# Two layers of mixed attention on one core: values projected with 512 weight columns per matmul, and half of each layer's memory values projected inside the two 16-head attentions

## The reference, cut to what matters

```python
m = rms_norm_2(mem, mem_norm_g)
for layer in range(DEPTH):
    ...
    h = h + memory_cross_attention(rms_norm_2(h, xa_norm_g[layer]), m, ...)

def memory_cross_attention(h, m, wq, wkv, wo):
    kv = m @ wkv
    k = kv[..., :D].reshape(B, -1, XA_HEADS, XA_HEAD_DIM)
    v = kv[..., D:].reshape(B, -1, XA_HEADS, XA_HEAD_DIM)
```

## Time and profile before

| | us |
|---|---|
| median of 3 runs | 1078.62 (1078.27 to 1079.88) |
| the profiled execution | 1080.66 |
| its span in the trace | 1078.9 |
| PE busy | 1039.4 (96%) |
| DVE busy | 693.4 (64%) |
| ACT busy | 535.6 (50%) |

### The profile page before, as it was taken

One profiled execution on the slowest core, in us unless ns is written; L12 is line 12 of the kernel. 1 busy time (PEld: TensorE's weight loads), 2 busy tenths in 40 slices (PEclk: granted clock), 3 DMA queues, 4 the chain that ended last, 5 costly groups with the idle time before them and its releaser, 6 DMA issues.

```text
span 1078.9 us, 19922 instructions
## 1 busy us (share of the span) xinstructions
PE 1039.4 (96%) x8144; PEld 1004.7 (93%) x8144; DVE 693.4 (64%) x1002; ACT 535.6 (50%) x822; POOL 226.1 (21%) x167
## 2 busy tenths in 40 slices
PE   8969999999999999999999999999999999999996
PEld 8959987999998899979999999899999999999996
DVE  5989976674446567646455658846576655658842
ACT  4325567365548546355435437644345545436631
POOL 3745201210004232001000103611024100102610
PEclk9979999999999999999999999999999999999998
DMA  9424532555540344515443455446545542555421
GB/s 347 154 86 146 196 118 88 186 195 195 195 162 35 121 155 178 217 58 194 167 147 109 170 190 194 154 169 245 205 164 209 181 156 81 193 190 180 148 106 39
DMA packets 26623, 173.27 MB, mean 161 GB/s; under 512 B 2880, under 2 KB 5184, under 8 KB 5952
## 3 DMA queue, kind: packets, MB, share of 16 engines
q1 hardware_dynamic: 24832, 161.26, 41.8%
q10 hardware_dynamic: 1728, 11.14, 2.7%
HBM read 167.15 MB, written 5.24 MB: 160 GB/s over the span
## 4 chain that ended last, share of the span: by engine, by line
PE 75%; DVE 13%; ACT 5%; issue 2%; POOL 2%; DMA 1%; SPq 0%; POOLq 0%; DVEq 0%; ACTq 0%
PE bank L373 63%; DVE wl L1163 5%; PE bank L479 2%; DVE work L1193 2%; DVE work L1477 2%; ACT wh L737 2%; PE bank L509 1%; POOL acc L1603 1%; DMA vec<-vecs 1%; DVE work L1480 1%; PE bank L499 1%; PE bank L441 1%; PE bank L511 1%; PE bank L600 1%; ACT work L1084 1%
## 5 line engine op out<-in xcount | busy, mean ns | idle before, releaser
L1163 DVE TENSOR_TENSOR wl<-raw,wh 128x1024 fp32r<-128x1024 f32 x300 | 394.9, 1324 | 251.0 <-ACT wh L737 249.3
L737 ACT ACTIVATE wh<-raw 128x1024 fp32r<-128x1024 f32 x300 | 312.9, 1054 | 302.9 <-PE bank L373 286.1
L373 PE MATMUL bank<-xh,wh 128*128 128x256 f32 x1312 | 367.3, 287 | 6.2 <-DVE wl L1163 4.1
L373 PE MATMUL bank<-xh,wl 128*128 128x256 f32 x1312 | 363.0, 283 | 0.0
L373 PE MATMUL bank<-xl,wh 128*128 128x256 f32 x1312 | 339.2, 284 | 0.0
L373 PEld LDWEIGHTS bank<-xh,wh 128*128 128x128 f32 x1312 | 252.1, 192 | 7.8 <-DVE wl L1163 4.8
L373 PEld LDWEIGHTS bank<-xh,wl 128*128 128x128 f32 x1312 | 252.3, 192 | 0.2
L373 PEld LDWEIGHTS bank<-xl,wh 128*128 128x128 f32 x1312 | 237.9, 192 | 0.1
L373 PE MATMUL bank<-yh,wh 128*128 128x256 f32 x768 | 210.6, 287 | 0.8 <-ACT yh L1088 0.8
L373 PE MATMUL bank<-yh,wl 128*128 128x256 f32 x768 | 208.5, 284 | 0.0
L373 PE MATMUL bank<-yl,wh 128*128 128x256 f32 x768 | 179.8, 285 | 4.2 <-POOL yl L1638 4.2
(11 more groups left out here) (156 smaller groups left out, 1307.3 us busy)
## 6 DMA issues: line engine op xcount, KB each, us to landing
raw<-w SPq DMA_DIRECT2D x149, 1024.0 KB, 4.8
k_scratch<-kt ACTq DMA_DIRECT2D x2, 1024.0 KB, 7.1
kt<-k_scratch ACTq DMA_DIRECT2D x2, 1024.0 KB, 6.3
cs<-cst SPq DMA_DIRECT2D x1, 1152.0 KB, 12.8
raw<-w SPq DMA_DIRECT2D x2, 512.0 KB, 6.3
h<-xt SPq DMA_DIRECT2D x1, 1024.0 KB, 7.2
v<-memt ACTq DMA_DIRECT2D x1, 1024.0 KB, 6.4
m_scratch<-yh ACTq DMA_DIRECT2D x1, 1024.0 KB, 6.1
```

Of the source, the lines that this page charges most:

```text
L373: return pe.matmul(b[:, j, :], lhs, rhs, start=k0 + k == 0 and q == 0 and (j == 0 or not both_open), stop=k0 + k == KT * p.deep - 1 and q ...
L737: act.activation(wh[:, n % 2, :, part], raw[:, n % RAW_SLOTS, :, part], ACT.Copy).then_inc(hi_ready, 1)
L1163: dve.tensor_tensor(wl[:, n % 2, :, part], raw[:, n % RAW_SLOTS, :, part], wh[:, n % 2, :, part].bitcast(F32), ALU.subtract).then_inc(lo_r ...
```

## The change

A new `project_tokens` takes all the phases that have tokens on partitions. Their weight chunks hold 512 rows by 512 columns instead of 1024 by 256. A matmul has the same stationary operand (128 tokens) and moves 512 weight columns, into a whole PSUM bank; a chunk has 24 of them. Both banks of the pair fill together (one for each 128 tokens), after two chunks. The halves of a chunk are now two row tiles each, both in the slot's layout and in what is waited for: the first half can be used when it alone is ready, and `w_used` rises after each half. ACT reads out one bank at a time. The second 512 columns of `va` and `vb` go to the same two banks, so their first matmul in a bank waits for that bank's read-out.

Columns 0 to 511 of the memory values of layer 0 and 1 become phases `vm0` and `vm1` of two chunks each. `project_piece` issues their 48 matmuls three at a time, one piece in each of the 16 turns of attention A and B, between the transposes (or the sums) and the values. ACT and DVE make the four halves (`filled_in`) in turns 2, 4, 8, 12 and 3, 5, 9, 13. ACT reads the result out at turns 18 and 19, sends it to DRAM (`v_scratch`, 512 KB each), and fetches it back before the cross attention. `oa` and `ob` now wait for that read-out in `enter`. `vx0` and `vx1` keep two chunks each, and the early read-out of `vx1` (`first_values`) is gone.

The very first weight chunk's two half transfers are contiguous in each partition (4 KB) instead of pieces of 512 bytes.

```diff
+            def project_tokens(name, oh, ol, ready=None, hooks={}, tile0=0):
+                p = PH[name]
+                enter(p)
+                for c in range(p.n):
+                    n = p.n0 + c
+                    slot = n % 2
+                    for half in range(2):
+                        pe.wait_ge(lo_ready, 2 * n + half + 1)
+                        if ready is not None and c < 2:
+                            hi_, lo_ = ready(4 * c + 2 * half)
+                            pe.wait_ge(*hi_)
+                            pe.wait_ge(*lo_)
+                        for t in range(2):
+                            if c >= 2 and c % 2 == 0 and half == 0:
+                                pe.wait_ge(evac[p.reader], p.base + c - 1 + t)
+                            for e in range(2):
+                                k = 4 * (c % 2) + 2 * half + e
+                                kk, part = tile0 + k, slice(t * P, t * P + P)
+                                for q in range(3):
+                                    mm = pe.matmul(bank[p.pair + t][:, :], (oh, oh, ol)[q][:, kk, part],
+                                                   (wh, wl, wh)[q][:, slot, half, e * 2 * CW:(e + 1) * 2 * CW],
+                                                   start=k == 0 and q == 0, stop=k == KT - 1 and q == 2,
+                                                   skip_group_check=True)
+                            if t == 1:
+                                mm.then_inc(w_used, 1)
+                            elif half == 1 and c % 2 == 1:
+                                mm.then_inc(tok_full, 1)
+                            if (c, half, t) in hooks:
+                                hooks[c, half, t]()
```

```diff
@@ TensorE, attention A @@
                     if 2 <= t < heads + 2:
                         turn(t - 2)
+                    if filler is not None and t < heads + 2:
+                        project_piece(filler, t - 2, yh, yl, KT)
                     if t == 3:
@@ TensorE, attention B @@
                 if 2 <= t < NH + 2:
                     z_sums(t - 2)
+                if t < NH + 2:
+                    project_piece("vm1", t - 2, yh, yl, KT)
@@ ScalarE @@
+            def filled_in(name, t):
+                p = PH[name]
+                for h_, at in ((2, 2), (3, 4), (4, 8), (5, 12)):
+                    if t == at:
+                        hi(2 * p.n0 + h_)
+                if t == 18:
+                    if name == "vm1":
+                        act.wait_ge(z_sp, NH)
+                    act.wait_ge(tok_full, TOKBASE[name] + 1)
+                    half_values(name, 0)
+                if t == 19:
+                    act.wait_ge(w_used, 2 * (p.n0 + p.n))
+                    half_values(name, 1)
+                    act.wait_ge(act_evac, p.end)
+                    act.dma_start(v_scratch[int(name[2])], v_half.rearrange("p t n -> p (t n)")).then_inc(v_saved, 16)
@@ ScalarE, values of A @@
-            def va(c, b):
-                if c == 2:
+            def va(c, t, b):
+                if c == 1 and t == 0:
                     spread("mem", rb_m)
@@ VectorE @@
+            def filled_in(name, t):
+                for h_, at in ((2, 3), (3, 5), (4, 9), (5, 13)):
+                    if t == at:
+                        lo(2 * PH[name].n0 + h_)
```

More of the change, by code:

```diff
@@ L77, in schedule, with add @@
     order = []
-    def add(name, chunks, reader, outs=None, deep=1):
+    def add(name, chunks, reader, outs=None, deep=1, wide=False):
         nonlocal at
@@ L86, in add @@
         count[reader] += p.outs
+        p.wide = wide
         p.pair = 2 * (len(order) % 2)
@@ L133 @@
 PH, NCHUNK = schedule()
+HALF = KT * P
 def bases(*uses):
@@ L142, in bases @@
     return table
+TOKBASE = bases(("va", 2), ("vm0", 1), ("vb", 2), ("vm1", 1), ("zf", 1), ("vn", 1), ("vx0", 1), ("vx1", 1))
 XBASE = bases(*[(u, 4) for u in ("first", "B", "mix0", "xa0", "ffn0", "mix1", "xa1", "ffn1")])
@@ new lines, in project_piece @@
+            def project_piece(name, i, oh, ol, tile0):
+                p = PH[name]
+                c, half, t, e = i // 8, i // 4 % 2, i // 2 % 2, i % 2
+                slot = (p.n0 + c) % 2
+                if i == 0:
+                    enter(p)
+                if t == 0 and e == 0:
+                    pe.wait_ge(lo_ready, 2 * (p.n0 + c) + half + 1)
+                k = 4 * c + 2 * half + e
+                for q in range(3):
+                    mm = pe.matmul(bank[p.pair + t][:, :], (oh, oh, ol)[q][:, tile0 + k, t * P:t * P + P],
+                                   (wh, wl, wh)[q][:, slot, half, e * 2 * CW:(e + 1) * 2 * CW],
+                                   start=k == 0 and q == 0, stop=k == KT - 1 and q == 2, skip_group_check=True)
+                if t == 1 and e == 1:
+                    mm.then_inc(w_used, 1)
+                elif e == 1 and half == 1 and c == 1:
+                    mm.then_inc(tok_full, 1)
@@ L749, in chunks @@
                             hi(2 * n + 3 + j)
-                    if c % p.deep == p.deep - 1 and evacuate is not None:
+                    if p.wide and evacuate is not None:
+                        if c % 2:
+                            for t in range(2):
+                                if t == 0:
+                                    act.wait_ge(tok_full, TOKBASE[name] + c // 2 + 1)
+                                else:
+                                    act.wait_ge(w_used, 2 * n + 2)
+                                evacuate(c // 2, t, bank[p.pair + t][:, :])
+                    elif c % p.deep == p.deep - 1 and evacuate is not None:
                         if p.reader == "act":
@@ L1266, in normalise, with soft_attention @@
                     dve.tensor_scalar(pr[:, at], pr[:, at], erec[:, u, q:q + 1], None, ALU.mult).then_inc(p_ready, 1)
-            def soft_attention(name, heads, bias, scale, extra, lag):
+            def soft_attention(name, heads, bias, scale, extra, lag, filler=None):
                 for t in range(2, heads + lag):
+                    if filler is not None:
+                        filled_in(filler, t)
                     if t < heads:
@@ L1763, in cols, with wide @@
     def cols(a, lo, hi):
-        return [tiled(a[r:r + D, c:c + CW]) for c in range(lo, hi, CW) for r in range(0, a.shape[0], D)]
+        return [tiled(a[r:r + D, c:c + CW]).reshape(P, KT, 2, P).transpose(0, 2, 1, 3).reshape(P, 2, HALF)
+                for c in range(lo, hi, CW) for r in range(0, a.shape[0], D)]
+    def wide(a, lo, hi):
+        return [tiled(a[r:r + D // 2, c:c + 2 * CW]).reshape(P, 2, HALF)
+                for c in range(lo, hi, 2 * CW) for r in range(0, D, D // 2)]
     wa, wb = x["w_in_a"][0], x["w_in_b"][0]
@@ L1776 @@
             chunks += cols(x["w_in_c_2"][0], 0, 3 * D)
-        chunks += cols(kv[l], D, 2 * D)
+        chunks += wide(kv[l], D + 512, 2 * D)
         if l == 1:
```

142 lines of the change are left out of this document (74 added, 68 removed).

## The result

| kernel | median us (lowest to highest) | ratio to before, 95% |
|---|---|---|
| before, the same runs | 1078.74 (1078.27 to 1079.88) | 1 |
| changed | 1072.77 (1072.37 to 1074.95) | 0.9947 (0.993 to 0.9964) |

The change makes the kernel 6.0 us faster, 0.5%. The forecast was 15.3 us. The time lies 9.5 us above the forecast one, 0.2 us inside the upper end of the range, and between rival 1 (1068.8) and rival 2 (1075.1). One run of the kernel before in a later group took 3144.56 us and is left out of that group's ratios. The profiled execution of the changed kernel took 1074.95 us with a span of 1073.1, against 1080.66 and 1078.9: 5.8 us of span.

A forecast was written before the change was run, and what follows sets the result against it. PE was taken to bound projections and attentions. Terms from -11.8 us for width to +1.2 for va's wait summed to -15.4 us, taking the profiled 1080.66 to 1065.3 and the median to 1063.3 us; range 1058 to 1073.

The forecast's parts named there:

- rival 1: Wide matmuls: each pays the fixed 0.013 us, so 0.227 us each, 5.5 us more, 1068.8 us; chance 0.18.
- rival 2: Wide matmuls: time goes per column, 0.240 us each, 11.8 us more, 1075.1 us; chance 0.07.
- What bounds the kernel: Projections and both attentions: PE, busy 96% of the span, bounds them; at the start the chain hangs on a constant.
- The width: All 20 token chunks: 480 matmuls of 512 columns at 0.2155 us replace 960 of 256 at 0.120; -11.8 us.
- The move: Attentions A and B: pieces lengthen turns by their own 0.65 us; A's start -1.2, B's edges -0.5, `oa` +0.1 us.
- rival 3: Attention turns: moved pieces fill idle time inside the turns, 12 us more gained, 1051.3 us; chance 0.07.
- rival 4: Attentions: splitting steps on ACT and DVE are on the path, 19 us lost if all exposed, 1082.3 us; chance 0.05.
- Finer waits: Chunks start on their first half: vx0 -1.1, zf -1.3, vx1 with `oc` -0.1 us (-1.4 to +2).
- The wait in va: Middle of va: second 512 columns wait for ACT's norm copy and bank read-out; +1.2 us (0.9 to 1.6).
- The start: Kernel start: faster first weight transfers land the awaited constant at 19.2 instead of 19.9 us; -0.7 us (0 to -1.5).

The follow-up runs named there:

- columns run: Changed kernel plus 132 extra matmuls behind gb, results unused: 24 each of 128 to 512 columns in fp32r, 12 each of 128 to 512 in fp32; 1109.46 us.
- run with doubled steps: Changed kernel with each of the 16 splitting steps put between softmax steps done two times; 1080.68 us, one run.

## Why the prediction was right and wrong

**What bounds the kernel: right.** PE stands alone in the chain of the turns in the middle of both attentions and of the long projections, before and after; at the ends of the attentions ACT and DVE are in it.

**The width: the step that failed.** "That looks like a floor of about 0.12 us for a weight load with its matmul, below which a short matmul cannot go and under which a long one does not fall" is the sentence. From it came 0.2155 us for a wide matmul and the -11.8 us; measured are 0.227 and -6.1. The three rows it stood on were read one way too many. That the 0.013 is absent at half clock was taken as proof that it is no fixed part; it can as well be a fixed part that only shows at full clock, and is. The two records of 8 columns were misread. They are one fp32 matmul (the code has one for each token tile, and its operands are fp32), and beside three of 0.120 they leave 0.58 - 0.36 = 0.22 us, 0.110 each; the mean of 0.116 hid that. The columns run has the same 0.222 us for an fp32 matmul of 128 columns. So the row itself put the floor at 0.110, below the 0.120 that it was to explain. And the Fourier records are fp32, which pays 0.005 to 0.009 for four passes. No row was of the disputed kind, fp32r over 256 columns. Rival 1 had the width's part right (0.227, 480 × 0.0115 = 5.5 us more); measured are 480 × 0.0117 = 5.6. With 0.18 it was given too little for something that no row excluded.

The width is 5.6 of the 9.5 us by which the forecast missed. The other 3.9 us are the terms below, less what the start and the end of the kernel gave; they are also why the time lies 4.0 us above rival 1. The forecast's bounds are also added wrongly: the start, vx1 and va allow -2.4 and +3.2 us, not -2.9 and +4; no term hangs on that.

**The move: right in kind.** Pieces of 0.70 (0.65 forecast, by the same rate) lengthen each turn by themselves; rival 3 is false by the turns, rival 4 by the turns too (PE alone in the chain, 0.70 longer) and by the run with doubled steps. What it cost at its edges was undersized: 0.9 for `oa` where 0.1 stood (0 to 1). The forecast knew that `oa` waits in `enter` and had ACT end with PE. ACT made both read-outs only behind the last piece, from 188.29 us, and ended 0.5 us after PE's last value (189.07); the other 0.46 us are the time between ACT's end and PE's start. In `ob` ACT did end with PE (385.23 and 385.26), and the 0.41 are that time alone. And 0.3 were lost in B where 0.5 gained was expected. In B the forecast let the last pieces hide in the wait for POOL at the last sums and in the wait for the last values; the first (0.36) is gone, but the second stays at 0.98 us as it was. The runs add that removing the waits of `oa` and `ob` gains nothing, so their size alone was not the miss; the end of an attention is as long as its last heads' chain.

**Finer waits: right**, vx0 -1.2 and zf -1.0. In vx1 the mechanism was right (POOL's low parts late next) and the size off: 2.06 us of PE waiting where 1.3 was written. Undoing the second layer's move takes this wait away and gives 1.0 us net.

**The wait in va: size right by luck.** The forecast had PE wait in the middle of va for the read-out of a bank behind the copy; no such wait is in the trace. It stands at the second scores, since ACT's copy follows the first exponentials and comes at the last read-out, not in the middle. The edit that moves the copy gained 1.1 with the pieces early and 1.3 with nothing moved.

**The start: right in kind**, 1.0 by the transfers where 0.7 was taken, and the constant landed at 18.7 us instead of 19.2. Between the two traces it is 1.2 (the selection stretch ahead of ka begins at 59.77 and 58.59 us) and another 0.5 in that stretch itself (15.60 and 15.10), which stands under half-level clock for most of its length.

**The clock: not in the sum.** 3.0 us of half-level stretches in kx0 and kx1 stand in both traces of the changed kernel. I had treated the granted clock as given. The last 63 us give 0.9 of these 3.0 back, and the selection stretch 0.5 if its gain is the clock's, so that the clock cost the changed kernel's trace 1.6 us net. The mean granted clock over the timed runs is the same for both kernels in one group (0.986 for 17 runs before, 0.986 for 6 after), so on average it should cost little; but the medians of the two kernels differ by 5.3 to 6.0 us, not by the 7.4 that would be left if the 1.6 were luck of two traces. How much of it recurs in most runs of the changed kernel stays open, and so does what decides which idle is followed by such a stretch.

## What to carry to other kernels

Count what a larger instruction saves as the fixed part alone, and price that part by a row of the same type at another size; where there is none, take the difference to pure streaming as paid by every instruction, and let the floor be the rival. Moving PE-bound work between PE-bound places is worth its waits and no more, and each phase put between two others changes whom the next one waits for. Differences of 1 to 3 us between two traces are to be set beside the granted clock before a cause is given to them.

## What the runs showed of the hardware

An fp32r matmul with its own weight load takes its columns at 2.4 GHz and 0.013 to 0.015 us (256 to 512 columns), and 0.110 us at 128 columns; a second one with the same stationary tokens, which is loaded again, pays the same. An fp32 one of four passes adds 0.005 to 0.009 us in all (128 and 256 columns), and takes 0.22 us at 8 columns as at 128. At the lower clock level the fixed part does not show (0.215 us for 256 columns). Between 80 us and the last projection each half-level stretch lasted 3.4 us; it cost 1.5 us under a streaming PE, and such stretches came and went with shifts of 0.9 us in otherwise equal kernels.
